# A new order for VectorE in the mix of a two-layer trunk: probabilities ahead of splits, signals for each head, convolutions beside the window units

## The reference, cut to what matters

```python
def token_mixing(h, lp, l, ctx_cache):
    proj = h @ lp['w_in']
    na_in, swa_in, hy_in, diff_in, gate_in = jnp.split(proj, list(SPLIT_IDX), axis=-1)
    ...
    a_o = neighbourhood_attention(na_q, na_k, na_v, ck_na, cv_na, lp['na_rpb'])
    b_o = window_attention(apply_rope(swa_q, tabs), ..., sink)
    d_o = diff_attention(rope_pair(d_q, tabs_d), ..., lam)      # softmax(map 0) - lam * softmax(map 1)
    d_o = rmsnorm(d_o, lp['diff_subln']) * (1.0 - lam_init)
    c_o = hyena(hy_in, lp)                                      # short convolution of 3 taps, then long ones by FFT
    ...
    for i in range(1, N_BRANCH):
        merged = merged + gates[:, :, i] * (branches[i] @ lp['w_branch'][i])
    return merged @ lp['w_out'], ctx_out
```

## Time and profile before

| | before |
|---|---|
| median of 3 runs | 2076.85 us |
| lowest, highest | 2075.71, 2079.9 us |
| profiled execution | 2080.09 us, span 2078.3 us |
| mean granted TensorE clock | 0.977 of full speed |
| busy in the span: PE, PEld | 1949.2 us (94%), 1868.2 us (90%) |
| DVE, ACT, POOL | 1442.3 us (69%), 787.5 us (38%), 446.3 us (21%) |

### The profile page before, as it was taken

How to read it: one execution, slowest core, us unless ns; L and a number is a source line. 1 busy time by engine, 2 the same in 40 slices (tenths; PEclk the granted TensorE clock), 3 DMA queues, 4 the chain that set the end, 5 groups by cost and what they waited for, 6 DMA issues and landing times.

```text
span 2078.3 us, 29068 instructions
## 1 busy us (share of the span) xinstructions
PE 1949.2 (94%) x11000; PEld 1868.2 (90%) x11000; DVE 1442.3 (69%) x2290; ACT 787.5 (38%) x1301; POOL 446.3 (21%) x359
## 2 busy tenths in 40 slices
PE   6999998999778999999999999989987799999998
PEld 6999997878668999999999999978876699999998
DVE  7888888566655457888888888865666544674444
ACT  3323234334333344332363333542444323533333
POOL 2301013212224521010131010321212353210102
PEclk9999999999979999999999999999999899999999
DMA  7767763223112235666566666432321123553332
GB/s 301 253 229 229 229 215 131 85 91 99 64 64 77 94 132 193 204 208 201 187 227 193 210 190 209 159 99 79 107 77 64 64 89 104 183 166 127 124 130 81
DMA packets 82832, 310.09 MB, mean 149 GB/s; under 512 B 9460, under 2 KB 10922, under 8 KB 81952
## 3 DMA queue, kind: packets, MB, share of 16 engines
q1 hardware_dynamic: 80064, 298.77, 43.6%
q0 software_dynamic: 2656, 9.85, 1.4%
HBM read 305.70 MB, written 2.88 MB: 148 GB/s over the span
## 4 chain that ended last, share of the span: by engine, by line
PE 80%; DVE 13%; ACT 4%; issue 2%; DMA 0%; SPq 0%; POOL 0%; DVEq 0%; ACTq 0%; POOLq 0%
PE bank L1479 44%; PE ps_att L1479 26%; PE ps_br L1479 2%; DVE pr L1274 1%; DVE lo L869 1%; PE ps_att L1732 1%; ACT hi L617 1%; PE ps_att L1723 1%; ACT pr L800 1%; DVE tiny L1253 1%; PE ps_o L1750 1%; DVE areaG L1304 1%; DVE pr L1277 1%; DVE areaO L989 1%; DVE areaE L1288 1%
## 5 line engine op out<-in xcount | busy, mean ns | idle before, releaser
L617 ACT ACTIVATE hi<-raw 128x1024 fp32r<-128x1024 f32 (+1 forms) x396 | 432.5, 1093 | 598.0 <-PE bank L1479 332.0
L869 DVE TENSOR_TENSOR lo<-raw,hi 128x1024 fp32r<-128x1024 f32 (+1 forms) x396 | 501.5, 1267 | 121.0 <-ACT hi L617 120.2
L1479 PE MATMUL bank<-h_hi,hi 128*128 128x384 f32 (+1 forms) x1536 | 543.9, 354 | 18.9 <-POOL h_lo L1377 8.7
L1479 PE MATMUL bank<-h_lo,hi 128*128 128x384 f32 (+1 forms) x1536 | 524.6, 342 | 0.0
L1479 PE MATMUL bank<-h_hi,lo 128*128 128x384 f32 (+1 forms) x1536 | 524.0, 341 | 0.0
L1479 PEld LDWEIGHTS bank<-h_hi,hi 128*128 128x128 f32 x1536 | 295.6, 192 | 49.2 <-issue 33.7
L1479 PEld LDWEIGHTS bank<-h_lo,hi 128*128 128x128 f32 x1536 | 295.8, 193 | 1.3
L1354 POOL TENSOR_TENSOR g_lo<-areaF,g_hi 128x384 f32 x88 | 109.6, 1245 | 868.2 <-ACT g_hi L696 868.2
L1479 PEld LDWEIGHTS bank<-h_hi,lo 128*128 128x128 f32 x1536 | 295.0, 192 | 0.0
L1479 PE MATMUL ps_att<-h_hi,hi 128*128 128x386 f32 (+1 forms) x736 | 248.7, 338 | 2.5 <-DVE lo L869 2.5
L1479 PE MATMUL ps_att<-h_hi,lo 128*128 128x386 f32 (+1 forms) x736 | 248.5, 338 | 0.0
(11 more groups left out here) (256 smaller groups left out, 2696.1 us busy)
## 6 DMA issues: line engine op xcount, KB each, us to landing
raw<-w_main SPq DMA_DIRECT2D x332, 512.0 KB, 4.1
areaM<-w_ada SPq DMA_DIRECT2D x134, 512.0 KB, 3.4
raw<-w_fused SPq DMA_DIRECT2D x64, 640.0 KB, 3.9
areaG<-w_ada SPq DMA_DIRECT2D x7, 512.0 KB, 12.4
areaO<-c_rep SPq DMA_DIRECT2D x3, 1024.0 KB, 5.9
areaE<-bias POOLq DMA_DIRECT2D x2, 1024.0 KB, 6.1
x<-x_in SPq DMA_DIRECT2D x1, 1536.0 KB, 9.0
areaE<-w_ada SPq DMA_DIRECT2D x3, 512.0 KB, 15.4
```

The costliest lines, as they stand in the source:

```text
L617: act.activation(hi[:, slot, 0:width(base)], raw[:, slot, 0:width(base)], ACT.Copy).then_inc(hi_ready, 1)
L869: dve.tensor_tensor(lo[:, slot, 0:w], raw[:, slot, 0:w], hi[:, slot, 0:w].bitcast(F32), ALU.subtract).then_inc(lo_ready, 1)
L1479: last = pe.matmul(dst, wt[:, slot, w], ac[:, c, 0:cols], start=c == 0 and k == 0, stop=c == chunks - 1 and k == 2)
```

## The change

It changes the plan's order and the grain of the signals; no arithmetic is added or dropped.

- Filter generator: one proj tile more beside it (15 instead of 14), 8 instead of 5 units of distance between the two sine layers; the filter, spectrum and conv steps 0 and 1 stand directly behind one another.
- NA: one unit instead of two before the rotations begin; vk and rope steps stand in pairs behind each "probs" step, instead of one behind each "scores" and one in the middle of each gap.
- NA and SWA: "probs" after 2.6 instead of 2.4 of the unit's 4.0; in SWA the short convolution follows it.
- DF: no short convolution; "probs" after 4.0, the turn 0.5 later; subinv and subout behind "probs".
- `staged()`: between "scores" and "probs" the feed is held back at a tile's last part, but never beyond the next tile's first part.
- Softmax: every VectorE instruction over both heads is split in two, with a signal per head; a DF unit puts the two maps of a head side by side in PSUM, so that the maxima of a head are one instruction.

```diff
-FILTER_TILES = 14
-NA_EARLY = 2
+FILTER_TILES = 15
+NA_EARLY = 1
...
         if kind == DF:
-            out += [1.0, ("short", w), 2.0]
+            out += [4.0, ("probs", kind, w)]
             if w == 4:
                 out += [("subinv", 0, b) for b in range(TB)]
             if w == 5:
                 out.append(("subout", 0))
-            out += [("probs", kind, w), 1.8, ("turn", kind, w)]
+            out += [0.5, ("turn", kind, w)]
...
-            out += [2.4, ("probs", kind, w), 1.6]
+            out += [2.6, ("probs", kind, w)]
+            if kind == SWA:
+                out.append(("short", w))
+            out.append(1.4)
             waiting = (kind, w)
...
-        if tile and s[-1] == PARTS - 1:
+        if tile and (s[-1] == 0 or s[-1] == PARTS - 1 and not chain):
             flush(fed)
...
-        if s[0] == "probs" or s[0] in ("proj", "out") and s[-1] == 1:
+        chain = s[0] == "scores" or chain and s[0] != "probs"
+        if s[0] == "probs" or s[0] in ("proj", "out") and s[-1] == 1 and not chain:
             flush(fed)
...
-    fil = [0.5, ("sinmlp", 0), 5.0, ("sinmlp", 1), 5.5]
+    fil = [0.5, ("sinmlp", 0), 8.0, ("sinmlp", 1), 5.5]
...
-        if isinstance(s, tuple):
-            rest.append(s)
-            if turns and s[0] == "scores":
-                rest.append(turns.pop(0))
-        elif turns:
-            rest += [s / 2, turns.pop(0), s / 2]
+        if turns and rest and isinstance(rest[-1], tuple) and rest[-1][0] == "probs":
+            rest += [0.3, turns.pop(0), 0.6, turns.pop(0), s - 0.9]
...
                         for hh in range(2):
-                            dst = pr[:, hh, 0:nk_]
-                            last = dve.tensor_scalar(dst, dst, rr[:, hh:hh + 1], None, ALU.mult)
+                            dve.wait_ge(exp_done, 2 * pair_no(l, ty, w) + hh + 1)
+                            rs, rr, dst = column(12, ty, w, hh), column(16, ty, w, hh), pr[:, hh, 0:nk_]
+                            if ty == SWA:
+                                link(dve.tensor_tensor(rs, rs, column(20, ty, w, hh), ALU.add))
+                            link(dve.reciprocal(rr, rs))
+                            last = dve.tensor_scalar(dst, dst, rr[:, 0:1], None, ALU.mult)
```

More of the change, by code:

```diff
@@ L246, in staged @@
 def staged(plan):
-    out, fed, gates = [], [], []
+    out, fed, gates, chain = [], [], [], False
     def flush(what):
@@ L279, in mix_plan @@
             fil += [("taps", o, tk), 3.3, ("tapsum", o, tk), 0.3]
-        fil += [("scale", o), 3.0]
-        for fc in range(TB):
-            fil += [("filter", o, fc), 0.8]
+        fil += [("scale", o), 3.0, ("filter", o, 0), ("filter", o, 1), 1.6, ("filter", o, 2), 0.8]
     proj = [("proj", k) for k in range(N_PROJ)]
@@ L310, in mix_plan @@
     for o in range(2):
-        hy += [("ytok", o, 0), 1.2, ("ytok", o, 1), 1.5]
-        for fc in range(TB):
-            hy += [("spectrum", o, fc), 0.8]
-        hy += [1.0, ("conv", o, 0), 0.8, ("conv", o, 1), 2.0]
+        hy += [("ytok", o, 0), 1.2, ("ytok", o, 1), 1.5, ("spectrum", o, 0), ("spectrum", o, 1), 1.6, ("spectrum", o, 2), 1.8,
+               ("conv", o, 0), ("conv", o, 1), 2.8]
     hy += [("hyout", 0), ("hyout", 1), 0.5]
@@ L791, in mix @@
                         nk_ = keys(b)[1] - keys(b)[0]
[L792 to L794 removed]
+                        for hh in range(2):
+                            act.wait_ge(max_ready, 2 * pair_no(l, ty, w) + hh + 1)
                             if ty == SWA:
[L797 to L801 removed]
+                                sink = column(20, ty, w, hh)
+                                act.activation(sink, sink, ACT.Exp).then_inc(sink_ready, 1)
+                            nm, rs = column(8, ty, w, hh), column(12, ty, w, hh)
+                            for m in range(2 if ty == DF else 1):
+                                dst = pr_2 if m else pr
+                                last = act.activation(dst[:, hh, 0:nk_], att(ty, w, hh, m)[:, 0:nk_], ACT.Exp, bias=nm[:, m:m + 1],
+                                                      accum_out=rs[:, m:m + 1])
                             last.then_inc(exp_done, 1)
@@ L1714, in mix @@
                         if pair_no(l, ty, w):
-                            pe.wait_ge(exp_done, round_no(l, ty, w))
+                            pe.wait_ge(exp_done, 2 * pair_no(l, ty, w))
                         pe.wait_ge(t_free, T_PER * l + turns_before(step))
                         k0, k1 = keys(b)
-                        for m in range(2 if ty == DF else 1):
-                            for hh in range(2):
+                        for hh in range(2):
+                            for m in range(2 if ty == DF else 1):
                                 a = 64 * hh + 32 * m
                                 e = a + (32 if ty == DF else 64)
-                                last = pe.matmul(ps_att[:, att_set(ty, w) + 2 * m + hh, 0:k1 - k0], q[a:e, blk, P * b:P * (b + 1)], kt[a:e, kb, k0:k1],
+                                last = pe.matmul(att(ty, w, hh, m)[:, 0:k1 - k0], q[a:e, blk, P * b:P * (b + 1)], kt[a:e, kb, k0:k1],
                                                  start=True, stop=True)
@@ L1731, in mix @@
                             for i in range((keys(b)[1] - keys(b)[0]) // P):
-                                last = pe.transpose(ps_att[:, att_set(ty, w) + hh, P * i:P * (i + 1)], pr[:, hh, P * i:P * (i + 1)], ident)
+                                last = pe.transpose(att(ty, w, hh)[:, P * i:P * (i + 1)], pr[:, hh, P * i:P * (i + 1)], ident)
                         last.then_inc(t_ready, 1)
```

55 lines of the change are left out of this document (18 added, 37 removed).

## The result

The changed kernel takes 2084.27 us in the median of 11 runs (2079.84 to 2086.19), the kernel before 2076.85 in 11: a ratio of 1.003, interval 1.0021 to 1.0039, 7.4 us slower. The forecast was 2088, slower, and 2064 to 2103. Its own range for the likeliest case, 2080 to 2095, holds the time. Of the terms that were added up, the cycle of C and the waits of B and D came near. A is right for the generator itself, but has the wrong sign when it is made alone. E, the clock, came near its +1 only as the net of a loss and a gain of 7 to 10 us each, neither of which had been worked out.

The account below looks back on a forecast made before the run. TensorE's own work was taken as the bound, leaving waits and clock to win. Terms: -4.1 + 2 x (5.7 + 6.1 - 4.6) + 1 = +11.3 on 2080.09, so 2091.4, or 2088 on the median; range 2064 to 2103.

Parts of the forecast that it names:

- likeliest case: Whole kernel: slower, forecast 2088 us, with 2080 to 2095 as its own range; chance 0.42.
- C: Window units: the added short convolution makes VectorE the bound, cycle 9.8 us; +6.1 us per layer, bounds -2.0 and +9.
- B: Neighbourhood units: second rotations of pairs wait for VectorE, 10.0 us for three pairs; +5.7 us per layer, bounds -0.4 and +7.5.
- D: Differential units: convolutions leave the chain, waits 21.3 us against 25.9; -4.6 us per layer, bounds -16 and +2.
- A: Filter generator: wider sine-layer distance covers waits; -4.1 us over both layers, between 0 and -6.0.
- E: TensorE's clock: fewer differential waits against long new ones in the other two stages; +1 us for both layers.
- Rival 3: Neighbourhood and window stages: new waits lower the clock to 0.93, 7.5 us per layer; 2103 us on the median; chance 0.10.
- Rival 2: Neighbourhood stage: second rotations wait no longer than 1.3 us, so no change; 2076 us on the median; chance 0.20.
- The estimate beside this step: Window units: by the skill page's 58-cycle fixed price, the head-wise split costs a third of 0.73 us; 2 us lower per layer.
- Rival 1: Differential units: POOL does not stretch the probabilities, about 11 us less per layer; 2065 us on the median; chance 0.28.
- Rival 4: Differential units: in three of six the probabilities do not precede the split; included in the forecast, no separate chance.
- The signs named for E: Trace after: clock near 0.85 from 535 us on and still 1.00 before.

Follow-up runs that it names:

- the filter run: The kernel before with only the filter generator's part of the change, including the moved tile and one early neighbourhood unit: 2093.82 us, ratio 1.007.
- the old rotations: The changed kernel with the old rule for vk and rope steps (one behind each scores step, one mid-gap) instead of pairs: 2061.17 us, ratio 0.9927.
- the run with the probabilities first: The changed kernel with feeds and gates held back in the plan until the probs step has been passed: 2061.72 us, ratio 0.993.
- the second profile: The changed kernel run again without edit, profiled in an execution of 2086.02 us; median 2084.99 us, ratio 1.0038.
- put right: The changed kernel with old vk/rope rule, differential probabilities before late gates and splits, short convolutions moved behind two differential turns and ahead of long ones: 2007.65 us, ratio 0.9655.
- the same over both heads: The kernel of 2007.65 us with softmax instructions and signals over both heads, as before the change: 2007.98 us, ratio 0.9665.

## Why the prediction was right or wrong

**A, filter generator: right for itself, wrong sign when made alone.** The step counted the waits of the generator (-4.1 for both layers). Up to the first neighbourhood scores, without the 4.17 us of the tile, both layers together take 6 us less in the filter run and 8 and 5 us less in the two profiles of the changed kernel (the slow stretch named at the end left out). But the step took the tile that the generator gets as free. In the old order it was not: with the tile gone, and the early unit that moves with it, the neighbourhood stage lost 7.6 us per layer. In the new order little of this is left: with the old rotations the stage takes 52.1 us against 51.8. The step never asked whose work the tile had hidden.

**B, neighbourhood units: right mechanism and right waits, the clock missing.** The second rotations wait 2.31, 3.54 and 4.01 us against 2.7, 3.65 and 3.65, and all waits of the stage grew by 5.4 us against 5.7. But the stage is 9.7 us longer (61.5 against 51.8), not 5.7. Missing is the term for the clock: 4.3 us per layer, from the rows of busy time. Rival 3 had this mechanism at 0.93 for both stages; it came in this one (0.92) and hardly in the window stage (0.97). Rival 2 is out: none of the pairs' waits is near 1.3. Also missing, on the other side: with the old rotations the new order, with its grain per head, takes this stage from 59.4 to 52.1 us, which I had counted as the 3.0 us of turns. So the whole loss of the change is the pairs; without them the same change is 15 us faster than the kernel before.

**C, window units: right.** The cycle is 9.63 us against 9.8 forecast, the stage 4.7 us longer against 6.1. The wait is not where it was put: the turns wait 1.2 us in sum, where 2 for each unit were named as the sign, and the branch matmuls 5.5, since the gate comes late with the rest of VectorE's row. Without the convolutions the stage is 6.4 us shorter, so they are its whole loss. The lower clock (0.97, 2.1 us more busy time) costs nothing here: with the old rotations the stage runs at 1.00, waits 8.1 us instead of 6.6 and is as long, since VectorE sets its pace:

```profile
478.90:534.30 55.40, 47.22 (x301) 39.54 (x298) 45.39 (x125) 22.93 (x62) 10.49 (x7) 1.00 0.26 88
```

The estimate beside this step, that C would be 2 us lower, and its sentence that the trace does not agree hold for one table row of the Trainium skill alone (VectorE: DVE Perf Modes, The TRN2 errata); the same section says that this row is too low for a single operation.

**D, differential units: right mechanism, gain of the waits a little too small, the clock missing.** Turns and gates together wait 19.1 us against 21.3 forecast and 25.9 before, units 2 and 4 5.46 each against 5.7, units 1 and 3 0.98 and 1.43 against 1.0 and 1.9, units 0 and 5 2.45 and 3.16 against 3.1 and 3.9. Rival 1 (no stretching) is out: the scalings stand at 1.03 and 1.50 us, and taking GpSimd's work away brings 2 us in units 2 and 4. (Its sum counts 23 us for twice 11; with 22 it lies at 2066.) Rival 4, that the order is not what it says in even units, was rightly put into the forecast, and the run with the probabilities first shows its price: 9 to 12 us per layer. But the stage became 10 to 14 us shorter in the first profile, not 4.6: 6.8 of it are waits, the rest is busy time of the same matmuls, since the clock rose from 0.82 and 0.86 to 0.91.

**E, clock: right in sum by luck, wrong in both parts.** I set it at +1 as a net of two unlike effects and worked out neither. Beside the rotations 4.3 us per layer are lost. In the differential units 3 to 7 us per layer are won (the busy time of the same matmuls: 77.44 and 73.64 us before, 70.57 and 70.67 after in the first profile, 73.65 in the second's layer 0 over the same cut). Over both layers the net is about -1.4 us in the first profile and +1.7 in the second. The signs named for E failed: the clock is 0.91 and not near 0.85 in the differential stage, and 0.92 and not 1.00 in the neighbourhood stage. The two parts are what B and D lack.

So the total came out near through errors that cancel, which is luck. Against their terms, for both layers and by the second profile, the neighbourhood stages are 8 us longer, the differential ones some 11 shorter, the window ones 3 shorter and the generator 1 shorter. On top come 1.4 us behind the first out tile of each layer, where a stretch of slow matmuls appears that the kernel before does not have. It is not explained: of two kernels with the same plan, the one put right and the same over both heads, the second has it and the first has not. Why the differential stage of layer 0 varies by 3.0 us between executions stays open too.

## What to carry to other kernels

A wait of TensorE is not priced by its length alone: here waits of 2 to 5 us cost up to as much again in slower matmuls behind them, and gave it back when they went; so price a stage by its busy time at either clock, not by the sum of its waits. A tile that is moved to cover one stage uncovers another. And when work is taken off a chain in an in-order queue, look where it lands: the convolutions paid 6.4 us in the window stage, 6.5 ahead of the first transposes, and no wait that a trace shows behind the turns and ahead of the long convolutions (no run has these two places alone).

## What the runs showed of the hardware

- With an equal sum of waits (10.6 to 10.8 us per layer in the neighbourhood stage) the clock was 0.92 with VectorE's instructions per head and 0.97 over both heads. In the window stage it was 0.97 with 6.6 us of waits (the changed kernel) and 1.00 with 8.1 us (old rotations). The sum of the waits does not give the clock.
- The stage of most waits before, 26.5 us of 104, ran at 0.82 and 0.86 in the two layers; put right, with 5.4 us of waits and the same matmuls, it ran at 0.95 and 1.00. TensorE's busy time there fell from 77.44 and 73.64 to 67.17 and 64.16 us with no instruction taken away.
